# Router logits from the sums ahead of the norm, token tile by token tile, in a two-layer decoder step

## The reference

```python
mix = jnp.concatenate([tok, m], axis=-1) @ P['w_out'][li]
x = layer_norm(ALPHA * x + mix, P['ln_mix_g'][li], P['ln_mix_b'][li])

def layer_norm(x, g, b):
    mu = jnp.mean(xf, axis=-1, keepdims=True)
    var = jnp.mean(jnp.square(xf - mu), axis=-1, keepdims=True)
    return ((xf - mu) * lax.rsqrt(var + LN_EPS)) * g + b

def hier_moe(x, w_group, b_group, w_router, b_router, w1, w3, w2):
    lg = xt @ w_group + b_group        # 4 groups
    le = xt @ w_router + b_router      # 16 experts
    ...                                # top group, top 2 experts in it, their products
```

## Time and profile before

| | us |
|---|---|
| median of 3 runs | 1222.47 (1221.97 to 1224.55) |
| the profiled execution | 1225.72 |
| its span, first to last instruction | 1223.8 |

### The profile page before, as it was taken

One profiled execution on the slowest core, in us unless ns is written; L12 is line 12 of the kernel. 1 busy time (PEld: TensorE's weight loads), 2 busy tenths in 40 slices (PEclk: granted clock), 3 DMA queues, 4 the chain that ended last, 5 costly groups with the idle time before them and its releaser, 6 DMA issues. The chain is left out here.

```text
span 1223.8 us, 22941 instructions
## 1 busy us (share of the span) xinstructions
PE 1060.8 (87%) x9246; PEld 641.7 (52%) x9246; DVE 410.6 (34%) x1092; ACT 261.5 (21%) x688; POOL 51.0 (4%) x61
## 2 busy tenths in 40 slices
PE   7999999999989999449998978997877995999950
PEld 5888888865473333148875644453453444333210
DVE  3233323454453212180010143444442336321118
ACT  2222212131012111061110112333352001111114
POOL 0000000000000000200000000000010001000011
PEclk9999999999999999769999989999796997999985
DMA  7964323738448999999999928999643705899944
GB/s 235 291 234 127 118 64 87 273 116 305 179 180 339 392 422 355 321 359 324 362 344 350 352 87 310 354 355 364 235 122 121 310 35 220 329 360 406 388 157 173
DMA packets 128185, 319.80 MB, mean 261 GB/s; under 512 B 9679, under 2 KB 67200, under 8 KB 118606
## 3 DMA queue, kind: packets, MB, share of 16 engines
q1 hardware_dynamic: 116078, 275.03, 62.5%
q0 software_dynamic: 7504, 27.45, 6.3%
q10 hardware_dynamic: 4496, 15.83, 3.2%
HBM read 288.31 MB, written 29.97 MB: 260 GB/s over the span
## 5 line engine op out<-in xcount | busy, mean ns | idle before, releaser
L1566 PE MATMUL bank<-W,XT 128*32 128x512 f32 x1408 | 158.5, 603 | 5.6 <-DMA W<-in_w13f 3.0
L1181 PE MATMUL bank<-WOUT,CAT 128*128 128x512 f32 x232 | 101.4, 594 | 0.6 <-PEq L434 0.5
L561 PE MATMUL bank<-XT,WH 128*128 128x260 f32 x448 | 100.4, 384 | 0.0
L1566 PEld LDWEIGHTS bank<-W,XT 128*32 128x32 f32 x1408 | 44.0, 111 | 104.3 <-issue 100.6
L2408 PE MATMUL bank<-XT,W 128*64 128x260 f32 x768 | 92.5, 396 | 5.7 <-DVE CAT L2683 3.2
L561 PEld LDWEIGHTS bank<-XT,WH 128*128 128x128 f32 x448 | 84.4, 190 | 13.5 <-issue 0.3
L561 PE MATMUL bank<-WH,XT 128*128 128x256 f32 x384 | 84.8, 379 | 0.0
L1597 PE MATMUL bank<-WD,GT 128*32 128x512 f32 x704 | 80.0, 595 | 1.6 <-DVE GT L1671 1.6
L561 PEld LDWEIGHTS bank<-WH,XT 128*128 128x128 f32 x384 | 72.1, 190 | 9.8 <-issue 0.4
L2408 PEld LDWEIGHTS bank<-XT,W 128*64 128x64 f32 x768 | 55.5, 141 | 38.4 <-issue 9.2
L1181 PEld LDWEIGHTS bank<-WOUT,CAT 128*128 128x128 f32 x232 | 43.4, 190 | 52.8 <-issue 52.5
(11 more groups left out here) (456 smaller groups left out, 1300.6 us busy)
## 6 DMA issues: line engine op xcount, KB each, us to landing
W<-in_w13f SPq DMA_DIRECT2D x32, 2048.0 KB, 12.7
PGS<-in_KP SPq DMA_DIRECT2D x128, 384.0 KB, 5.3
PGS<-in_VP SPq DMA_DIRECT2D x128, 384.0 KB, 5.3
WD<-in_w2f SPq DMA_DIRECT2D x32, 1024.0 KB, 15.3
WH<-in_w_a SPq DMA_DIRECT2D x13, 1024.0 KB, 10.0
WOUT<-in_w_out SPq DMA_DIRECT2D x3, 2048.0 KB, 10.9
YS<-CAT ACTq DMA_DIRECT2D x12, 512.0 KB
W<-in_w_b SPq DMA_DIRECT2D x6, 1024.0 KB, 11.2
```

Of the source, the lines that this page charges most:

```text
L561: last = nc.tensor.matmul(PB[u["bank"]][:, 0:u["w"]], u["lhsT"](w, k), u["rhs"](w, k), start=(k == 0), stop=(k == KC - 1))
L1181: last = nc.tensor.matmul(PB[2 * (i % 2) + c][:, :], CAT[:, k, t * P:(t + 1) * P], w_out(c)[:, k, :], start=(k == 0), stop=(k == KC - 1))
L1566: last = nc.tensor.matmul(PB[2 + g % 2][32 * j:32 * j + 32, :], XGT[:, g % 2, k, 32 * j:32 * j + 32], W13[:, LANES[l][g][j] % WRING, k, :] ...
```

## The change

PE's result ahead of the norm, s, is what is transposed now. The logits are r * (s @ (g * W) - mu * sum(g * W)) + (sum(b * W) + bias): the gains are folded into the weights, and mu and r come in per token afterwards. In both layers:

- PE transposes the gains and biases (16 small transposes into bank 7), DVE multiplies the router's weights by them (`WRG`), PE sums both products over the channels with a matrix of ones (16 products with 20 columns), and DVE keeps the sums (`GW`).
- In each tile PE does the first half output, the transposes of the tile before (each half as soon as its residual is read), half of the second half output, the logits of the tile before, and the rest. The logits have the token tile as weights and stream the 20 columns of `WRG`, so they come out in token rows, in bank 6 or 7, and turning them back goes. In the first two tiles the preparation takes the place of this.
- DVE takes each half's residual and statistics by themselves, and norms a tile in place only after its transposes are made; the logits of a tile get their factors (`tile_logits`, two operations) in the turn of the next, those of the last tile at the start of the routing.

The logits of tile i wait for the folded weights where i < 2 (`gain_ready`), for the first half's copy in `XT` at k = 0 (`xh_out`) and for the second's at k = 4 (`xt_out`). ScalarE's turn of a tile is: wait for its variance, the deviation, then for each half wait for its transposes and copy them, wait for the norm, store to `XN`. The core of the diff, for PE:

```diff
+def gains():
+    pe.wait_ge(ln_in, 64 * l + 32)
+    for c in range(2):
+        for k in range(KC):
+            last = nc.tensor.transpose(PB[7][:, (c * KC + k) * NB:(c * KC + k + 1) * NB],
+                                       GB[0:NB, c, k * P:(k + 1) * P], const("ident", 0, NB, 0, NB))
+    last.then_inc(gain_ready, 1)
+def gain_sums():
+    pe.wait_ge(gain_ready, 4 * l + 2)
+    for c in range(2):
+        for k in range(KC):
+            last = nc.tensor.matmul(PB[7][:, 256 + 20 * c:276 + 20 * c], const("ones"), WRG[:, c, k, :], ...)
+    last.then_inc(gain_ready, 1)
+def logits(i):
...
+        last = nc.tensor.matmul(PB[6 + i % 2][0:r, t * 20:(t + 1) * 20], XT[:, k, t * P:t * P + r], WRG[:, 0, k, :], ...)
+    last.then_inc(lgt_ready, 1)
+for i in range(NT):
+    first = H if l == 0 and i == 0 else 0
+    if i >= 2:
+        pe.wait_ge(mm_used, 2 * (m0 + i - 1))
+    output(i, 0, range(first, KC)).then_inc(mm_ready, 1)
+    if i == 1:
+        gains()
+    if i > 0:
+        turned(i - 1)
+    if i < 2:
+        output(i, 1, range(first, KC)).then_inc(mm_ready, 1)
+    else:
+        output(i, 1, range(4))
+        logits(i - 1)
+        output(i, 1, range(4, KC)).then_inc(mm_ready, 1)
+    if i == 1:
+        gain_sums()
+        logits(0)
+turned(NT - 1)
+logits(NT - 1)
```

For VectorE, in the turn of tile i (before: both halves' residual, then `norm_steps`; on VectorE's side `gains` makes the products with `WR` and `gain_sums` reads the sums into `GW`), and for the start of the routing:

```diff
+for c in range(2):
+    dve.wait_ge(mm_ready, 2 * (m0 + i) + c + 1)
...
+    last.then_inc(mm_used, 1)
+    if i == 1 and c == 0:
+        gains()
+    dve.wait_ge(mm_used, 2 * (m0 + i) + c + 1)
+    last = nc.vector.bn_stats(st[:, 6 * c:6 * c + 6], xh)
+link(last)
+nc.vector.bn_aggr(st[:, 12:14], st[:, 0:12]).then_inc(var_ready, 1)
+if i == 1:
+    gain_sums()
+if i > 0:
+    dve.wait_ge(lgt_ready, m0 + i)
+    tile_logits(nc, dve, i - 1, order[i - 1], LOG[0:rows(order[i - 1]), order[i - 1], :])
+dve.wait_ge(var_ready, n0 + i + 1)
+dve.wait_ge(xt_ready, n0 + i + 1)
...
-for t in range(NT):
-    last = tt(LG[0:r, t, :], PB[2][0:r, t * 20:(t + 1) * 20], bias[0:r, :], ALU.add)
+dve.wait_ge(lgt_ready, NT * (l + 1))
+nc.vector.tensor_copy(LG[:, 0:PT - 1, :], LOG[:, 0:PT - 1, :])
+nc.vector.tensor_copy(LG[0:NB, PT, :], LOG[0:NB, PT, :])
+link(tile_logits(nc, dve, NT - 1, PT - 1, LG[:, PT - 1, :]))
```

More of the change, by code:

```diff
@@ L1147, in output_and_norm @@
                 m0 = NT * l
[L1148 to L1149 removed]
+                order = tile_order(l)
                 def w_out(c):
@@ L1170, in _, with output @@
                     def _(pe):
+                        def output(i, c, steps):
+                            t = order[i]
+                            for k in steps:
+                                if t < PT:
+                                    last = nc.tensor.matmul(PB[2 * (i % 2) + c][:, :], CAT[:, k, t * P:(t + 1) * P],
+                                                            w_out(c)[:, k, :], start=(k == 0), stop=(k == KC - 1))
+                                    continue
+                                for j in range(4):
+                                    last = nc.tensor.matmul(PB[2 * (i % 2) + c][32 * j:32 * j + NB, 0:P], CAT[:, k, SEQ:TOK],
+                                                            w_out(c)[:, k, j * P:(j + 1) * P], start=(k == 0), stop=(k == KC - 1))
+                            return last
@@ new lines, in turned @@
+                        def turned(i):
+                            t = order[i]
+                            r = rows(t)
+                            if i > 0:
+                                pe.wait_ge(xt_out, n0 + i)
+                            for c in range(2):
+                                pe.wait_ge(mm_used, 2 * (m0 + i) + c + 1)
+                                for k in range(4):
+                                    last = nc.tensor.transpose(PB[4 + c][:, k * P:k * P + r],
+                                                               X[0:r, t, (4 * c + k) * P:(4 * c + k + 1) * P], const("ident", 0, r, 0, r))
+                                last.then_inc((xh_ready, xt_ready)[c], 1)
@@ new lines, in gains @@
+                        def gains():
[6 more added lines that the diff above has]
+                        def gain_sums():
+                            pe.wait_ge(gain_ready, 4 * l + 2)
+                            for c in range(2):
+                                for k in range(KC):
+                                    last = nc.tensor.matmul(PB[7][:, 256 + 20 * c:276 + 20 * c], const("ones"), WRG[:, c, k, :],
+                                                            start=(k == 0), stop=(k == KC - 1))
+                            last.then_inc(gain_ready, 1)
@@ L1171, in _ @@
                         if l == 1:
                             pe.wait_ge(wout_in, 32)
[L1173 to L1189, removed]
@@ L1192, in logits @@
[L1192 to L1201, removed]
@@ L1203, in _ @@
[L1203 to L1211, removed]
```

98 lines of the change are left out of this document (64 added, 34 removed).

## The result

The changed kernel takes 1249.49 us (median of 4, 1247.62 to 1256.05) beside 1223.51 for the kernel before (median of 4, 1221.97 to 1227.75): a ratio of 1.0209, interval 1.0181 to 1.0237. It is slower, as predicted, but by 26 us instead of 12, outside the range. The profiled execution took 1247.62 us, with a span of 1245.8; PE is busy 1078.6 us (before 1060.8) with 9332 instructions (9246), the mean granted clock is 0.927 (0.935).

What follows compares the result with a forecast made beforehand. TensorE was taken to bound the output passes, with VectorE over half free. Layer 1's +5.5 and layer 0's +6.65 gave +12.1 us on the profiled execution, 1237.8; on the median 1234.6 (stated as 1234.5), range 1226 to 1239.

Steps and rivals of the forecast that it cites:

- the sum of layer 1: Layer 1's output stage and routing start: 11.46 us added ahead of T0, tail 6.1 shorter, routing +0.15; +5.5 us.
- T0: End of a layer's last output pass, where the tail begins; forecast 19.4 us later in layer 0, 11.46 in layer 1.
- the bound of 6.3: Upper price in us of a layer's sums over the folded weights, at 1.2 GHz for most of it; 3.55 taken.
- one row, behind an idle time: Layer 0's tail before: TensorE idle 2.94 us at 331.9, then the low clock with 2.8 us of loss.
- The clock in layer 0: Low clock behind TensorE's 3.05 us wait for the gains ahead of the sums: 2.8 us lost, bounds 0 and 2.9.
- What is behind shifts with the routing: After each output stage: only +0.15 us at the routing's start; later weight loads and the last store at zero.
- third rival: Tails: the store behind the norm or a low clock holds the routing 1 to 2 us a layer; about 1238, 10%.
- the price of 0.11 us a pass: Logits and sums: a pass loading 128 weight columns and streaming 20 costs 0.111 us; 16 passes take 1.78.
- the first rival: Logits and sums: the weights' load hides, a pass costs 0.029 us; 3.9 us faster in all, 1218.6; chance 8%.
- the exchange of operands that saves nothing: A tile's logits with tokens as weights: 1.78 us against 1.92 now; only the turning back goes, 0.6 a layer.
- the tail of 5.8 us: From T0 to routing in both layers: 5.75 us, ended by the norm and its store; 18.65 and 11.85 before.
- the direction of both layers: Both layers slower: +6.65 us in layer 0, +5.5 us in layer 1.

Runs made afterwards that it cites:

- a_wide: Changed kernel with the sums over the folded weights streaming 128 columns a pass instead of 20, same 32 passes; 1241.71 us, ratio 1.0132 to the kernel before.
- a_pad85: Changed kernel with 85 more unused short TensorE products where it waits behind the experts of layer 0; 1250.26 us, one run.
- b_t0late: Kernel before, with SyncE in layer 0 asking for experts' weights 1 and 2 only behind the last tile's logits; 1225.98 us, ratio 0.9999.
- a_again: Changed kernel, unchanged, run once more; 1251.75 us, one run.
- b_again: Kernel before, unchanged, run once more; 1222.10 us, one run.
- b_code: Kernel before, with ten unused 8-column identity products between layer 0's last logits and their turning; 1230.36 us, ratio 1.0033.
- b_delay: Kernel before, with ten unused 512-column identity products between layer 0's last logits and their turning, holding back the routing; 1233.70 us, ratio 1.0070.
- b_act: Kernel before, with ScalarE in layer 0 taking the next tile's deviation ahead of copying out a tile's transposes; 1224.93 us, ratio 0.9992.
- a_sums2: Changed kernel with VectorE first adding the folded weights over the chunks, so the sums take 2 passes instead of 32; 1235.27 us, ratio 1.0094.

## Why the prediction was wrong

**The step that failed first** is the sum of layer 1: "In front of T0 now come: gains 1.2, sums 3.55, sample logits 0.5 ..." has no term for the clock; the bound of 6.3 was for the sums alone. From start to start the sums took 3.92 us (+0.4), but behind them the half output took 9.64 instead of 6.97 (+2.7), with PE never idle: 3.1 of the 3.4 us that layer 1 was off, the other 0.3 in the tail. I had read the low clock off one row, behind an idle time, and took idleness for its cause; a_wide shows that it is not the only one: with the same passes and a longer stream the half output takes 7.13 again. The Trainium skill, "TensorE: Matmul & The Clock Gate", section "HAM oscillation — how this bites in real kernels", ties the lower clock to gaps in which TensorE idles; layer 1 here differs (busy 8.00 of 8.00 us, clock 0.57), and the measurement decides.

**The clock in layer 0** was mis-sized: 2.8 taken, up to 2.9 allowed. The sums began when VectorE was ready, as forecast, though PE waited only 1.34 us and not 3.05, since the samples' second half already ran slowly (3.41). Then, from start to start, the sums took 5.28 (3.55 at full clock), the first logits 3.42 (1.78) and the half output 8.67 (6.97): 5.1 us lost. The 2.3 over my 2.8 are the 2.2 by which T0 moved further (21.6 instead of 19.4). The mechanism was only half right. a_wide, with an idle time of 2.95, loses some 1.7 us in its sums (5.30 from start to start, 3.55 at full clock) and nothing behind them; most of the loss in a_pad85 and, as far as the runs tell, here goes with the short stream, as in layer 1. That the third tile starts where I put it (302.7 on the scale of the kernel before, 302.4 forecast) is luck: a wait half as long, and a low clock that came later than I had it.

**"What is behind shifts with the routing"** gave 0.15 us to all that follows a stage. What it put at zero by name was right: the late weights cost nothing (b_t0late), and the first gather follows its indices as closely as before. But between the layers 4.0 us came that the sentence has no term for: 2.1 at a burst whose pauses the longer program of PE moved, of which the product behind gave 1.1 back; some 0.75 by my third rival's mechanism (the memory product at low clock ahead of the rank product); 2.9 at one store, with no cause shown; 0.7 came back later.

**Right**: the price of 0.11 us a pass against the 0.029 of the first rival, the exchange of operands that saves nothing, the tail of 5.8 us ended by the norm and its store, and the direction of both layers. The work put where PE has no cover, less what the tails gave back for it, is 9.4 us of the two stages (8.75 + 8.8, less 5.1 and 3.1 lost to the clock), where the forecast had 9.1 (6.5 + 5.35, less 2.8).

The medians differ by 26.0 and the two profiles by 21.9: the profiled run was the fastest of its four, and the stretch between the layers alone varies by 6 us. Where the other 4 us of the medians lie no profile shows.

## What to carry to other kernels

Before you move work ahead of a stage's last pass, look at what covers it now: logits that seemed to lie in a tail lay beside VectorE's norm, and moved between output passes they cost their full time. Price a burst of short products twice, once for its passes and once for the clock of the long product behind it, and replace it where VectorE can make the sum (32 passes to 2 gave 14 us here). A longer program moves TensorE's pauses in later bursts; allow a term of a microsecond or two either way, not zero, and look whether the product behind gives it back.

## What the runs showed of the hardware

- TensorE's clock fell from 2.4 to 1.2 GHz without an idle time, in passes that load 128 columns and stream 20 (layer 1, clock 0.57 behind them; 9.80, 8.45 and 8.61 us for the product after in the three profiles: after, a_again, a_pad85), and not in the same number of passes with 128 columns streamed (1.00 and 7.13 us, one profile, a_wide).
- The same idle time of 2.94 us ahead of the logits of layer 0 in the kernel before was followed by 7.70, 7.47, 7.36, 5.82 and 5.82 us for the same 64 passes in five profiles (before, b_again, b_code, b_t0late, b_delay): a low clock behind a wait is a chance, not a price.
- Passes with 128-column loads cost the same with 20 and with 128 streamed columns (from start to start 3.58 us for 32 in a_again and 3.66 in a_wide).
- TensorE pauses for 1.4 (b_act) to 3.7 us (before) every 126 to 128 passes in a burst of 384 short ones, and how many passes come ahead of the first pause moves with the length of its program: 204, 190, 184 and 160 where it is 0, 13, 20 and 43 passes longer (before, a_sums2, b_code, after).
